# Splitting the memory keys' projection into high and low halves, in a two-block transformer kernel on one core

## What is computed

```python
def memory_cross_attention(h, mem_n, xq_w, xkv_w, xo_w):
    q = (h @ xq_w).reshape(B, S, XATTN_HEADS, XATTN_HEAD_DIM)
    kv = (mem_n @ xkv_w).reshape(B, N_MEM, 2, XATTN_HEADS, XATTN_HEAD_DIM)
    k, v = kv[:, :, 0], kv[:, :, 1]
    ...

def second_block(...):
    mem_n = rmsnorm(mem, norm_mem_w)
    h = h + head_group_mixer(rmsnorm(h, norm_mix_w), positions, w_in, conv_w, ...)
    h = h + memory_cross_attention(rmsnorm(h, norm_xattn_w), mem_n, xq_w, xkv_w, xo_w)
    h = h + sq_relu_mlp(rmsnorm(h, norm_mlp_w), mlp_up_w, mlp_down_w)
```

## Time and profile before

| what | value |
|---|---|
| median of 3 runs | 1059.12 us (1058.96 to 1060.35) |
| span of the profiled execution | 1056.1 us; its own device time isn't listed apart from the runs |
| instructions | 21171 |
| TensorE (PE) busy | 1019.6 us, 97% |
| VectorE (DVE) busy | 688.7 us, 65% |
| ScalarE (ACT) busy | 508.4 us, 48% |
| chain that ended last | PE 87%, DVE 7%, ACT 3% |
| mean granted TensorE clock | 0.991 |

### The profile page before, as it was taken

How to read it: one execution, slowest core, us unless ns; L and a number is a source line. 1 busy time by engine, 2 the same in 40 slices (tenths; PEclk the granted TensorE clock), 3 DMA queues, 4 the chain that set the end, 5 groups by cost and what they waited for, 6 DMA issues and landing times.

```text
span 1056.1 us, 21171 instructions
## 1 busy us (share of the span) xinstructions
PE 1019.6 (97%) x8000; PEld 982.2 (93%) x8000; DVE 688.7 (65%) x1252; ACT 508.4 (48%) x832; POOL 31.1 (3%) x49
## 2 busy tenths in 40 slices
PE   4999999999999999999999999999999999999996
PEld 4999999989987789999999999887899999999996
DVE  4666664555676548776666548979666378885543
ACT  5544453363455545655444448341664365543431
POOL 4200000010100000000000000000000000000000
PEclk8999999999999999999999999999999999999998
DMA  6445465437732224655556456313454255556551
GB/s 218 160 178 172 167 230 178 150 118 237 239 120 92 90 80 141 200 193 185 180 200 232 166 184 214 120 61 120 165 174 141 100 180 183 191 184 199 169 189 42
DMA packets 46544, 172.71 MB, mean 164 GB/s; under 512 B 5498, under 2 KB 7682, under 8 KB 45968
## 3 DMA queue, kind: packets, MB, share of 16 engines
q1 hardware_dynamic: 44160, 162.58, 45.1%
q0 software_dynamic: 1360, 8.57, 2.5%
q10 hardware_dynamic: 960, 0.67, 0.2%
HBM read 170.72 MB, written 3.77 MB: 165 GB/s over the span
## 4 chain that ended last, share of the span: by engine, by line
PE 87%; DVE 7%; ACT 3%; issue 2%; DMA 1%; DVEq 0%; ACTq 0%
PE bank L384 26%; PE bank L386 25%; PE bank L385 25%; DVE cy L1291 3%; DVE wlo L365 1%; ACT whi L354 1%; PE bank L396 1%; PE bank L1089 1%; PE bank L779 1%; PE bank L781 1%; DMA res<-in_res 1%; PE bank L1474 1%; PE bank L1451 1%; PE bank L753 1%; PE bank L752 1%
## 5 line engine op out<-in xcount | busy, mean ns | idle before, releaser
L384 PE MATMUL bank<-xhi,whi 128*128 128x256 f32 (+1 forms) x1464 | 423.3, 289 | 10.9 <-DVE wlo L365 10.2
L386 PE MATMUL bank<-xhi,wlo 128*128 128x256 f32 (+1 forms) x1464 | 416.4, 284 | 0.0
L385 PE MATMUL bank<-xlo,whi 128*128 128x256 f32 (+1 forms) x1464 | 415.4, 284 | 0.0
L365 DVE TENSOR_TENSOR wlo<-raw,whi 128x1024 fp32r<-128x1024 f32 (+1 forms) x287 | 362.9, 1266 | 24.1 <-ACT whi L354 23.8
L354 ACT ACTIVATE whi<-raw 128x1024 fp32r<-128x1024 f32 (+1 forms) x287 | 311.5, 1086 | 129.6 <-PE bank L386 110.8
L384 PEld LDWEIGHTS bank<-xhi,whi 128*128 128x128 f32 x1464 | 277.4, 189 | 18.4 <-issue 17.5
L385 PEld LDWEIGHTS bank<-xlo,whi 128*128 128x128 f32 x1464 | 277.7, 190 | 0.2
L386 PEld LDWEIGHTS bank<-xhi,wlo 128*128 128x128 f32 x1464 | 277.4, 189 | 0.0
L384 PE MATMUL bank<-hid_hi,whi 128*128 128x256 f32 (+1 forms) x608 | 172.9, 284 | 0.0
L385 PE MATMUL bank<-hid_lo,whi 128*128 128x256 f32 (+1 forms) x608 | 172.6, 284 | 0.0
L386 PE MATMUL bank<-hid_hi,wlo 128*128 128x256 f32 (+1 forms) x608 | 171.8, 283 | 0.0
(11 more groups left out here) (258 smaller groups left out, 1163.5 us busy)
## 6 DMA issues: line engine op xcount, KB each, us to landing
raw<-in_w_f1in SPq DMA_DIRECT2D x44, 512.0 KB, 3.5
raw<-in_w_f2in SPq DMA_DIRECT2D x44, 512.0 KB, 3.5
raw<-in_w_mix SPq DMA_DIRECT2D x35, 512.0 KB, 3.5
raw<-in_w_up SPq DMA_DIRECT2D x32, 512.0 KB, 3.6
raw<-in_w_down SPq DMA_DIRECT2D x32, 512.0 KB, 4.1
raw<-in_w_f1out SPq DMA_DIRECT2D x16, 704.0 KB, 4.1
raw<-in_w_f2out SPq DMA_DIRECT2D x16, 704.0 KB, 4.2
raw<-in_w_mixb SPq DMA_DIRECT2D x20, 512.0 KB, 3.5
```

What stands on the lines that cost most here:

```text
L365: nc.vector.tensor_tensor(wlo[:, s, 0:tiles * P], raw[:, s, 0:tiles * P], whi[:, s, 0:tiles * P], ALU.subtract).then_inc(w_lo, 1)
L384: nc.tensor.matmul(out, whi[:, s, w], rhs_hi(t), start=start and t == 0, stop=False)
L385: nc.tensor.matmul(out, whi[:, s, w], rhs_lo(t), start=False, stop=False)
L386: mm = nc.tensor.matmul(out, wlo[:, s, w], rhs_hi(t), start=False, stop=stop and t == tiles - 1)
```

## The change

The eight `memk` chunks are treated like all others. ScalarE splits them (in steps 17 to 24) and so does VectorE; TensorE runs `strip` on them with `mem_hi` and `mem_lo`, 24 matmuls a step, in place of 8 plain ones. The scaled memory is no longer written back: in steps 4 to 11 ScalarE writes the scaled value straight into `mem_hi`, without the wait for the square, and in steps 5 to 12 VectorE writes `mem_lo` from `mem`, the gain and `mem_hi`. The two lines that made them in the attention stage are gone. A raw buffer is always freed by the split of its chunk. The exceptions for `plain` disappear.

```diff
@@ -93,13 +93,10 @@
     first, sizes, banks, need = plan()
     C = len(sizes)
     counts = {name: n for name, n, *_ in PHASES}
-    plain = range(first["memk"][0], first["memk"][0] + KT)
-
-    def splits(c, like=None):
-
-        at = c if like is None else like
-        assert at not in plain
-        return c + 1 - (len(plain) if at > plain[0] else 0)
+
+    def splits(c):
+
+        return c + 1
 
     ctx = ExitStack()
     with ctx:
@@ -344,7 +341,7 @@
 
             static = isinstance(i, int)
             c = c0 + per * i + j
-            if static and (c >= C or c in plain):
+            if static and c >= C:
                 return
             s = (c if static else c0 + j) % RING
             tiles = sizes[c] if static else sizes[c0 + per + j]
@@ -498,7 +495,7 @@
 
             def body(i, edge):
                 for j in range(4):
-                    pe.wait_ge(w_lo, splits(c0 + 4 * i + j, c0 + j))
+                    pe.wait_ge(w_lo, splits(c0 + 4 * i + j))
                     out = start_group(pe, g0, 4, i, j)
                     head = edge and i == 0 and j == 0
                     strip(out[:, 0:width], (c0 + j) % RING, KT, hi, lo,
@@ -1074,20 +1071,15 @@
         def pe_mixb(pe):
             for q in range(STEPS):
                 s = (sc + q) % RING
-                if q < 20:
-                    pe.wait_ge(w_lo, splits(sc + q))
-                else:
-                    pe.wait_ge(w_in[s], ((sc + q) // RING + 1) * 16)
+                pe.wait_ge(w_lo, splits(sc + q))
                 out = start_group(pe, sgrp, 1, q, 0)
                 if q < 20:
                     hi, lo = x_rhs("packed")
                     mm = strip(out[:, 0:NX], s, KT, hi, lo, before=wait_x(pe, N_MIXB) if q == 0 else None)
                 else:
                     if q == 20:
-                        pe.wait_ge(m_scaled, KT)
-                    for t in range(KT):
-                        mm = nc.tensor.matmul(out[:, 0:NX], raw[:, s, t * P:(t + 1) * P], mem[:, t, :], start=t == 0,
-                                              stop=t == KT - 1)
+                        pe.wait_ge(m_lo, KT)
+                    mm = strip(out[:, 0:NX], s, KT, lambda t: mem_hi[:, t, :], lambda t: mem_lo[:, t, :])
                 mm.then_inc(pe_done, 1)
                 if q == 0:
                     pe_stat(pe, N_MIXB, False)
@@ -1210,8 +1202,7 @@
                     if e >= 2:
                         act.wait_ge(m_stat, e - 1)
                     nc.scalar.activation(msq[:, e % 2, :], mem[:, e, :], ACT.Square).then_inc(m_sq, 1)
-                    act.wait_ge(m_sq, e + 1)
-                    nc.scalar.activation(mem[:, e, :], mem[:, e, :], ACT.Copy, scale=gain(N_MEM, e)).then_inc(m_scaled, 1)
+                    nc.scalar.activation(mem_hi[:, e, :], mem[:, e, :], ACT.Copy, scale=gain(N_MEM, e)).then_inc(m_hi, 1)
                 if q < 8 and q % 2 == 0:
                     act.wait_ge(acc_free, sgrp + q + 1)
                     nc.scalar.activation(sg[:, 0:NX], tg[:, 0:NX], ACT.Sigmoid).then_inc(cb_sig, 1)
@@ -1311,6 +1302,11 @@
                     nc.vector.tensor_tensor(hd[:, 0:NX], ps[6 + e % 2][:, 0:NX], sinv[:, :], ALU.mult).then_inc(rot_step, 1)
                     dve.wait_ge(rot_step, 3 * e + 2)
                     nc.vector.tensor_tensor(qr[:, e, :], qr[:, e, :], hd[:, 0:NX], ALU.add).then_inc(rot_step, 1)
+                if MEM0 < q <= MEM0 + KT:
+                    e = q - MEM0 - 1
+                    dve.wait_ge(m_hi, e + 1)
+                    nc.vector.scalar_tensor_tensor(mem_lo[:, e, :], mem[:, e, :], gain(N_MEM, e), mem_hi[:, e, :],
+                                                   ALU.mult, ALU.subtract).then_inc(m_lo, 1)
                 if q == 14:
                     dve.wait_ge(m_sd, 1)
                     nc.vector.reciprocal(col_inv[:, 0, 0:2], col_root[:, 0, 0:2]).then_inc(m_inv, 1)
@@ -1416,7 +1412,7 @@
                         mm = strip(out, s, KT, hi, lo, before=wait_x(pe, N_XATT) if m == 0 else None)
                     else:
                         mm = strip(out, s, KT, lambda t: mem_hi[:, t, :], lambda t: mem_lo[:, t, :],
-                                   before=(lambda t: pe.wait_ge(m_lo, t + 1)) if m == KT else None)
+                                   before=None)
                     mm.then_inc(pe_done, 1)
                 if m == 0:
                     pe_stat(pe, N_XATT, False)
@@ -1481,8 +1477,6 @@
                     split_hi(act, qc, 1, m, LEAD)
                 if m == 0:
                     act_norm(act, N_XATT, False)
-                if m < KT:
-                    nc.scalar.activation(mem_hi[:, m, :], mem[:, m, :], ACT.Copy).then_inc(m_hi, 1)
                 if m % 2 == 1 and 0 <= (m - 3) // 2 < XHEADS:
                     act_xexp(act, (m - 3) // 2)
                 if KT + 2 <= m < XSTEPS + 2:
@@ -1532,10 +1526,6 @@
                     dve_xmax(dve, (m - 2) // 2)
                 if 0 < m < XSTEPS:
                     split_lo(dve, qc, 1, m, LEAD)
-                if m < KT:
-
-                    dve.wait_ge(m_hi, m + 1)
-                    nc.vector.tensor_tensor(mem_lo[:, m, :], mem[:, m, :], mem_hi[:, m, :], ALU.subtract).then_inc(m_lo, 1)
                 if m % 2 == 1 and 0 <= (m - 3) // 2 < XHEADS:
                     dve_xprobs(dve, (m - 3) // 2)
                 if m % 2 == 0 and 0 <= (m - 12) // 2 < XHEADS:
@@ -1635,10 +1625,8 @@
                     static = isinstance(i, int)
                     c = c0 + 4 * i + j
                     last = c - RING
-                    if static and last in plain:
-                        sp.wait_ge(pe_done, last + 1)
-                    elif not (static and c < RING):
-                        sp.wait_ge(w_lo, splits(last, None if static else c0 + j))
+                    if not (static and c < RING):
+                        sp.wait_ge(w_lo, splits(last))
                     sp.dma_start(raw[:, (c0 + j) % RING, 0:tiles * P], w[4 * i + j]).then_inc(w_in[(c0 + j) % RING], 16)
 
                 for j in range(4):
```

More of the change, by code:

```diff
@@ L284, in build @@
         rot_mm, rot_step, rg_done = sem("rot_mm"), sem("rot_step"), sem("rg_done")
-        m_scaled, m_hi, m_lo, m_sq, m_stat, m_sd, m_inv, m_bc, m_r = (
-            sem(s) for s in ("m_scaled", "m_hi", "m_lo", "m_sq", "m_stat", "m_sd", "m_inv", "m_bc", "m_r"))
+        m_hi, m_lo, m_sq, m_stat, m_sd, m_inv, m_bc, m_r = (
+            sem(s) for s in ("m_hi", "m_lo", "m_sq", "m_stat", "m_sd", "m_inv", "m_bc", "m_r"))
         rv_tr, rv_copied = sem("rv_tr"), sem("rv_copied")
@@ L363, in split_lo @@
             tiles = sizes[c] if static else sizes[c0 + per + j]
-            dve.wait_ge(w_hi, splits(c, None if static else c0 + per + j))
+            dve.wait_ge(w_hi, splits(c))
             nc.vector.tensor_tensor(wlo[:, s, 0:tiles * P], raw[:, s, 0:tiles * P], whi[:, s, 0:tiles * P],
@@ L592, in body @@
                     q, m = j % cpm, j // cpm
-                    pe.wait_ge(w_lo, splits(c0 + per * i + j, c0 + j))
+                    pe.wait_ge(w_lo, splits(c0 + per * i + j))
                     if q == 0:
@@ L1572, in body @@
                 for j in range(4):
-                    pe.wait_ge(w_lo, splits(uc + 4 * i + j, uc + j))
+                    pe.wait_ge(w_lo, splits(uc + 4 * i + j))
                     out = start_group(pe, ug, 4, i, j)
```

## The result

The changed kernel takes 1067.24 us (median of 4 runs, 1063.63 to 1069.91) against 1059.73 us before (4 runs). The ratio is 1.007, with a 95% interval of 1.0047 to 1.0093: about 7.5 us slower. Five more executions beside eleven of the kernel before gave 1068.55 against 1059.25 us, ratio 1.0087 (1.0074 to 1.01).

What follows compares the result with a forecast made beforehand. VectorE was taken to lead in steps 5 to 12 and 20 to 24, TensorE elsewhere. 3.2 - 0.6 + 4.6 - 1.2 = +6.0 us plus 1.7 for the clock, 1059.1 + 7.7 = 1066.8 us; range 1063.0 to 1069.8.

Steps and rivals of the forecast that it cites:

- DVE leads in steps 5 to 12 and 20 to 24, PE between and at the end: Changed stage: VectorE sets the pace in steps 5 to 12 and 20 to 24, TensorE in 13 to 20, 26 and 27.
- Low halves, +3.2 us: Steps 5 to 12: eight memory low halves of 0.40 us each on VectorE, without slack, all passed on: 3.2 us more.
- Splits, four that count, +4.6 us: Steps 17 to 24: eight more VectorE weight splits; only those of steps 20 to 23 count, 4 x 1.14 = 4.6 us.
- one of the prediction's signs of being wrong: VectorE's waits were to cover the splits of steps 17 to 19; their pushing step 20 would show the forecast wrong.
- PE's saving of 0.6 us a step in the three steps where it leads: Steps 20, 26 and 27: split matmuls replace plain ones on TensorE, saving 3 x 0.6 = 1.8 us.
- Four passes against three, 1.0 us a step: Plain FP32 step by the four-pass rule: 4.04 us, saving 1.0 us a step; the sum used 0.6 instead.
- Nothing gained in the attention stage, ScalarE has room: Removing both halves from the attention stage gains nothing, TensorE being full; ScalarE can take eight splits of 1.06 us each.
- The clock, one fall, +1.7 us: After about 6 us idle, TensorE's clock falls once to half, over the mean's matmuls and step 26: 1.7 us more.
- behind step 13 in some executions: Two-falls rival: the clock also falls around step 13 and TensorE carries it through steps 14 to 16, 1.7 us; chance 0.20.
- The wait of step 25: TensorE's idle stretch before line 1176 of the last head pair grows from 1.37 to about 6 us.
- The first residual: Line 627, start of the next phase, comes 7.7 us later than before, and the end too.
- The 3.0 us outside the span: Median 1059.12 us less span 1056.1 us: these 3.0 us lie outside the span and stay.

Runs made afterwards that it cites:

- The two parts run alone: Kernel before with only the memory's low halves made early, 1064.23 us; kernel before with only the memory-key weight splits, which nobody reads, 1065.1 us.
- the narrow splits: Changed kernel with VectorE making the low half of each memory-key chunk over 32 of its 1024 columns only: 1062.35 us.
- the twins with fewer taps: Changed kernel and kernel before, both with a quarter of the convolution taps left out and five a step: 1052.78 and 1054.46 us.
- the kernel with unused splits: Kernel before with memory-key weights also split in steps 17 to 24, while TensorE still multiplies the plain weights: 1065.1 us.
- late filling: Changed kernel with 16 unused matmuls behind step 23 and 36 behind step 25, where TensorE idles: 1064.12 us.

## Why the prediction was right, point by point

*DVE leads in steps 5 to 12 and 20 to 24, PE between and at the end.* Right. The first line 1154 matmul comes 2.8 us later than before, measured from the same start (676.81 - 639.45 against 676.26 - 641.68), within the 2.8 to 3.2 us forecast. The two parts run alone, and the narrow splits, put the time in the same places.

*Low halves, +3.2 us.* Right: where the splits are narrow, the read of step 20 is 2.6 us late, which is 3.2 - 0.6. The experiment with them alone (8 x 0.34 = 2.7 us) gives 3.8 us with a clock fall.

*Splits, four that count, +4.6 us.* Right in sum, not quite in place. By the read of step 24 the kernel is 7.1 us late (741.94 - 639.45 against 95.37); the terms 3.2 - 0.6 + 4.6 give 7.2. But at the read of step 20 it was late by 3.0 us and not by 2.6. With narrow splits it is 2.6, so the splits of steps 17 to 19 weren't wholly covered: DVE came to that read 0.4 us after PE had finished. That they push step 20 was one of the prediction's signs of being wrong; it cost nothing, because DVE's next instruction had waited 0.42 us for PE before and no longer does.

*PE's saving of 0.6 us a step in the three steps where it leads.* Right: 1.2 us for the last two. That the other five are worth about the same once DVE is out of the way is what the profiles of the twins with fewer taps say (4.5 us for all eight); their medians differ by 1.7 us.

*Four passes against three, 1.0 us a step.* The measurement decides for 0.6: step 27 takes 755.52 - 752.50 = 3.0 us in the chain after, against 748.91 - 745.31 = 3.6 before.

*Nothing gained in the attention stage, ScalarE has room.* Right; PE is busy 8.00 of 8.00 us in both. From the first residual to the end of the span the profile after takes 300.0 us and the one before 300.9, but the kernel with unused splits, which still makes the halves in the attention stage, takes 299.9 as well, so these 0.9 us aren't a gain from their removal.

*The clock, one fall, +1.7 us.* The mechanism was right and its size wrong. The stretch at half clock around line 1130 was taken to cost as much as the one at 235 us, 3.2 us long, or the end of the one at the start, some 4 us; it lasted 6.7 us and cost 2.9 us. There were more falls than one: near 732 us, behind the wait of 2.21 us that the prediction didn't see, where the slower matmuls only filled PE's waiting and cost nothing; and behind step 13 in some executions, where it cost 1.0 us and not 1.7. The terms give 6.0 us without the clock, 2.9 us for the late fall and 1.0 us in some executions, 8.9 to 9.9 us. The stage is longer by 8.8 and 9.6 us in the two profiles, and the two comparisons of medians gave 7.5 and 9.3 us. The profiled execution of before ran at 1.00 through the whole stage. Of the eleven executions of before beside the second comparison, those with mean clocks of 0.991 and 0.992 have spans of 1056.6 to 1057.4 us and those at 0.988 have 1058.7 and 1059.0. So the kernel before loses time to falls of its own in some executions; that this is the whole rest is argued and not shown. The wait of step 25 was forecast at about 6 us and was 4.36, because the first fall made the matmuls of step 24 end later: they ran at half clock from 731.6 to 734.9 us, which costs about 1.4 us by the earlier trace rows. With late filling, the wait is 1.52 us behind 36 matmuls of 0.12 us, 5.8 us together. The first residual was forecast 7.7 us later and came 8.8 us later from the same start. So the number came out at 1066.8 against 1067.24 partly by luck: the clock term was too small, and the kernel before wasn't charged with any.

*The 3.0 us outside the span.* Wrong: executions that list both show 1.8 us (1063.63 - 1061.8). By that, the profile before was of an execution about 1.2 us below the median (1059.12 - 1.8 - 1056.1). It cost the forecast nothing, as shifts were added to the median.

## What to carry to other kernels

An engine that is busy for 97% of the span can still be waiting where you make its work cheaper. Before pricing a change, ask of each step which engine's instruction releases the next; a saving counts only there, and work moved to the engine that leads counts in full there (here 3.2 and 4.6 us). When a schedule by hand gives one engine background work, look for the steps in which that engine waits and put it there: the same taps at other steps gained 4 us, nearly what the edit to the matmuls would have brought (4.8 us) if each of its eight steps had been on the path.

## What the runs showed of the hardware

- The clock fell to 0.50 not only behind a wait of 4.36 us but also behind one of 2.21 us, and at 678.6 us of the second profile behind waits of 0.69 us for the transposition and 0.69 us for the scores. In the first profile the same two waits were followed by no fall (1.00 from 676 to 684 us). A fall cost 1.0 us (3.4 us long) and 2.9 us (6.7 us long) where PE's results were waited for, and nothing that the profile shows where PE waited for DVE anyway. 52 matmuls that compute nothing, 6 us of work in idle time, went with a median 4.4 us lower.
- GpSimd's elementwise instructions slow DVE's. A tap with two operands in the local memory took 478 ns alone and 612 ns on average with GpSimd at work beside it; GpSimd itself, with DVE at work beside it, needed 1307 ns on average for a multiplication of 128x256 by a scalar and 800 ns for an addition. The Trainium skill, page "GPSIMD Engine Reference", section "1. Specifications", says that its interfaces are shared with VectorE and that VectorE's instructions with two SBUF inputs contend; the rows agree and give the size.
